# Weight units split in pairs of 2048 columns in the plain stages of a decoder layer

## What is computed

```python
h = x + 1/2 * post1(SwiGLU_1(pre1(x)))
u = pre_mix(h);  P = u @ W_in
m = (sig(g1)*y_gla + sig(g2)*y_gdn + sig(g3)*y_xa) @ W_out
h = h + post_mix(m)
h = h + 1/2 * post2(SwiGLU_2(pre2(h)))
```

## Time and profile before

| | us |
|---|---|
| time, median of 3 runs | 2432.47 |
| lowest and highest | 2431.55, 2433.93 |
| time of the profiled execution | 2433.06 |
| its span, first to last instruction | 2431.3 |
| busy PE / DVE / ACT / POOL | 2410.6 / 1840.5 / 1336.8 / 440.0 |

### The profile page before, as it was taken

How to read it: one execution, slowest core, us unless ns; L and a number is a source line. 1 busy time by engine, 2 the same in 40 slices (tenths; PEclk the granted TensorE clock), 3 DMA queues, 4 the chain that set the end, 5 groups by cost and what they waited for, 6 DMA issues and landing times.

```text
span 2431.3 us, 32326 instructions
## 1 busy us (share of the span) xinstructions
PE 2410.6 (99%) x10933; PEld 1998.5 (82%) x10933; DVE 1840.5 (76%) x2219; ACT 1336.8 (55%) x1613; POOL 440.0 (18%) x867
## 2 busy tenths in 40 slices
PE   8999999999999999999999999999999999999998
PEld 7888888888888888888888888888888888888886
DVE  6999999987566456677676464465689999998885
ACT  6555555554555556657575444444655555555553
POOL 5211212201222003223242020010112121121000
PEclk9999999999999999999999999999999999999999
DMA  7777767767778765555665677676667777676665
GB/s 243 213 215 214 221 207 218 213 208 223 226 240 257 199 188 157 170 160 159 170 183 159 200 208 195 211 238 191 209 207 220 211 215 217 208 223 211 197 204 193
DMA packets 306063, 498.53 MB, mean 205 GB/s; under 512 B 28460, under 2 KB 102320, under 8 KB 305200
## 3 DMA queue, kind: packets, MB, share of 16 engines
q1 hardware_dynamic: 282336, 457.85, 62.7%
q0 software_dynamic: 23344, 38.95, 5.0%
q10 hardware_dynamic: 288, 0.52, 0.1%
HBM read 471.39 MB, written 8.52 MB: 197 GB/s over the span
## 4 chain that ended last, share of the span: by engine, by line
PE 92%; POOL 2%; DMA 2%; DVE 2%; SPq 1%; issue 1%; ACT 0%; DVEq 0%; POOLq 0%; ACTq 0%
PE acc L770 40%; PE acc L858 39%; PE mix L858 9%; POOL mkh L733 1%; DMA sq<-mk_scratch 1%; POOL mkh L730 1%; PE acc L795 1%; DMA post_a<-n_ffn_post 1%; SPq L438 0%; SPq L472 0%; PE mix L1082 0%; DVE wlo L1971 0%; PE acc L813 0%; PE mix L831 0%; PE mix L1128 0%
## 5 line engine op out<-in xcount | busy, mean ns | idle before, releaser
L1289 ACT ACTIVATE whi<-raw 128x1024 fp32r<-128x1024 f32 x860 | 902.3, 1056 | 972.4 <-PE acc L770 480.0
L1823 DVE TENSOR_TENSOR wlo<-raw,whi 128x1024 fp32r<-128x1024 f32 x568 | 687.3, 1228 | 322.8 <-ACT whi L1289 312.2
L1971 DVE TENSOR_TENSOR wlo<-raw,whi 128x2048 fp32r<-128x2048 f32 x146 | 333.6, 2285 | 54.1 <-ACT whi L1289 54.1
L770 PE MATMUL acc<-whi,u_hi 128*128 128x512 f32 x896 | 356.9, 398 | 0.0
L770 PE MATMUL acc<-whi,u_lo 128*128 128x512 f32 x896 | 349.4, 390 | 0.0
L770 PE MATMUL acc<-wlo,u_hi 128*128 128x512 f32 x896 | 349.1, 390 | 0.0
L387 POOL DMA_DIRECT2D nat<-nat x416 | 203.5, 498 | 791.9 <-DVE nat L2058 649.0
L858 PE MATMUL acc<-whi,x_hi 128*128 128x512 f32 x860 | 334.7, 389 | 0.3 <-DVE nat L1926 0.3
L858 PE MATMUL acc<-wlo,x_hi 128*128 128x512 f32 x860 | 334.6, 389 | 0.0
L858 PE MATMUL acc<-whi,x_lo 128*128 128x512 f32 x860 | 334.6, 389 | 0.0
L770 PEld LDWEIGHTS acc<-whi,u_lo 128*128 128x128 f32 x896 | 168.2, 188 | 35.8
(11 more groups left out here) (476 smaller groups left out, 3848.7 us busy)
## 6 DMA issues: line engine op xcount, KB each, us to landing
raw<-w_ffn_gu SPq DMA_DIRECT2D x352, 512.0 KB
raw<-w_ffn_down SPq DMA_DIRECT2D x176, 512.0 KB
raw<-w_in SPq DMA_DIRECT2D x224, 256.0 KB
raw<-w_in SPq DMA_DIRECT2D x96, 512.0 KB
raw<-w_mem_kv SPq DMA_DIRECT2D x32, 512.0 KB
raw<-w_out SPq DMA_DIRECT2D x32, 512.0 KB
nat<-nat POOLq DMA_DIRECT2D x416, 32.0 KB, 3.5
raw<-w_in SPq DMA_DIRECT2D x64, 128.0 KB
```

What stands on the lines that cost most here:

```text
L770: ins = nc.tensor.matmul(acc[:, par, t, :], x[:, k0 + k, cols], w[:, k, :], start=first and k == 0 and m == 0, stop=last and k == UK - 1 a ...
L1289: act(whi[:, l % RING], raw[:, l], ACT.Copy).then_inc(hi_ready, 1)
L1823: tt(wlo[:, l], raw[:, l], whi[:, l % RING].bitcast(fp32), ALU.subtract).then_inc(lo_ready, 1)
L1971: tt(wlo[:, g:g + 2], raw[:, g:g + 2], whi[:, g % RING:g % RING + 2].bitcast(fp32), ALU.subtract).then_inc(lo_ready, 2)
```

## The change

On ACT, `split_two` is new: at every second slot (odd j) it waits for both loads and for `unit_used` of that slot, and makes the upper parts of two neighbouring units in one copy of 2048 columns. It is used at all slots of the plain stages, and in the pair stages for the pairs that are not sevens. At the even slots ACT now only does the tasks. On DVE the plain stages use `split_pair` at odd slots in place of `split` at each. The sevens stay single on both engines.

```diff
+            def split_two(n, per_i, j):
+
+                i, n0, per = per_i
+                if isinstance(n, int):
+                    l, loads = (n + LOOK) % RAW, (n + LOOK) // RAW + 1
+                else:
+                    l, loads = (n0 + j + LOOK) % RAW, i * (per // RAW) + ((n0 + j + LOOK) // RAW + 1)
+                for s in (l - 1, l):
+                    ac.wait_ge(raw_full[s], loads * LOADED)
+                ac.wait_ge(unit_used, n + 1)
+                act(whi[:, (l - 1) % RING:(l - 1) % RING + 2], raw[:, l - 1:l + 1], ACT.Copy).then_inc(hi_ready, 2)
+
             def slots(n0, i, per, tasks, until=None):
 
                 for j in range(per):
-                    if until is None or j + LOOK < until:
-                        split(at(n0, i, per, j), (i, n0, per), j)
+                    if j % 2 and (until is None or j + LOOK < until):
+                        split_two(at(n0, i, per, j), (i, n0, per), j)
                     tasks(j)
...
-                split(n, per_i, j)
+                if s is not None:
+                    split(n, per_i, j)
+                elif j % 2:
+                    split_two(n, per_i, j)
...
                 for j in range(per):
                     tasks(j)
-                    if until is None or j + LOOK < until:
-                        split(at(n0, i, per, j), j)
+                    if j % 2 and (until is None or j + LOOK < until):
+                        split_pair(at(n0, i, per, j), j)
...
             def split_pair(n, j):
 
-                g = (j + LOOK) % RAW - 1
+                g = ((n if isinstance(n, int) else j) + LOOK) % RAW - 1
```

## The result

The changed kernel takes **2516.06 us** (median of 4 runs, 2515.55 to 2519.5) against 2432.14 us of the kernel before (4 runs in the same rounds, 2431.55 to 2433.93): ratio 1.0345, 95% interval 1.0333 to 1.0357. That is 84 us slower, where 44.5 were forecast, and above the range. The profiled execution took 2519.5 us, its span 2517.8, 86.5 more than the span before; the trace is read against this number.

What follows compares the result with a forecast made beforehand. PE, busy 2410.6 of 2431.3 us, was taken as the bound, so each new PE wait is paid in full. Late pairs summed to 44.5 us on the profiled 2433.06, 2477.6, given as 2477 us; range 2455 to 2508.

Steps and rivals of the forecast that it cites:

- The question is whether a unit's lower part is still there when PE comes to it: Whole kernel: PE's new waits are paid in full; what ACT and DVE save in work is not the question.
- The latency of a pair, 4.50 of 5.44 us: Slots without tasks: pair ready 4.50 us after its slot is free, PE wants it at 5.44; spare falls 5.6 to 0.9.
- Busy time of DVE and ACT lower by some 45 and 75 us: Sign to look for in the whole trace: both engines less busy by these amounts, the span longer all the same.
- Mixer, slot 1, 12.8: Proj groups 1 to 3 and gates0: the pair behind the convolution 3.2 us late each time, 12.8 in all.
- `lower_turned`, 5.7: Second half of down1, two odd slots: the pair 2.8 us late at each, 5.7 in all.
- Mixture parts, 5.0: Slot 19 of up0 and up1, slot 7 of gates1: 1.7 us late each, 5.0 in all.
- The same holds for the 60 sevens of gu1 and gu2; cost nothing: Pair right behind each seven in gu1 and gu2: just in time, spare some 0.2 us, cost nothing.
- Sevens in the first halves of down, 7.3: First halves of down1 and down2: five places in each, 0.73 us late, 7.3 in all.
- Steps of slots 18, 20 and 22, 1.6, bounds 0 and 10: Mixers: DVE's tasks stand behind a pair and PE's next small step waits, 0.4 us a group, 1.6 in all.
- First chunks of gu1 and gu2, mem, out, 12.1: Slot 1 of gu1 and gu2 2.5 us each, 6.0 with gu1's slots 9 and 11; mem 3.4 and out 2.7 estimated.
- The clock falls: Rival, chance 0.13: six of the long PE waits bring half clock, some 3 us each, 18 more: 2495 us.
- The upper end takes in both slower rivals but not their sum: Range's upper end, 2508 us: covers more late steps (2501, chance 0.20) or the clock's fall (2495, chance 0.13).

Runs made afterwards that it cites:

- slot1_single: Changed kernel, but slots 0 and 1 of the four groups with a mixer split singly on ACT and DVE: 2501.37 us, ratio 1.0276.
- pair_first: Changed kernel with DVE's pair ahead of its task in five slots (lower_turned twice, mixture parts three times): 2501.06 us, ratio 1.0280.
- late_singles: Changed kernel with ACT's copy single at chunk ends of gu1 and gu2 and two pairs behind each seven of down's first halves: 2493.13 us.
- where_free: Kernel before, with pairs on both engines only in plain slots whose tasks leave time, 119 pairs: 2434.80 us, ratio 1.0009.
- dve_singles: Changed kernel, but in the plain stages DVE makes two single subtractions after the odd slot's tasks in place of a pair: 2486.87 us.
- hold8: Kernel before, with eight extra DVE additions ahead of the subtraction at four slots of proj group 0, to make PE wait: 2451.32 us.
- plain_only: The change in the plain stages alone, on ACT and DVE, with ACT single in the pair stages: 2487.74 us, ratio 1.0213.

## Why the prediction was wrong

The direction, the reason and the largest term were right; the sum was half of the loss, 42 us short. Of these, 12.8 are the half clock and 11.8 the chunk ends of gu1 and gu2, both of which the sum held at nothing; 8.1 the down halves, 6.0 the other steps of the mixers, 3.4 the first chunks with mem and out, 1.1 the mixture parts and `lower_turned`; slot 1 of the mixers came out 1.2 below. Two of the signs of being wrong that it named came true: PE waits in the chunks of gu1 and gu2 with sevens, and matmuls in mid-kernel stand 0.43 apart. By its own steps:

- *"The question is whether a unit's lower part is still there when PE comes to it"*: right. PE waits on lower parts for 49.2 us. Proj group 0 has no tasks and loses 0.00.
- *The latency of a pair, 4.50 of 5.44 us*: nearly right. The copy was 0.03 us longer and DVE's start behind it 0.07 later, so the spare is 0.8 and not 0.9 us. Small, but it is paid at each of some 50 places.
- *Busy time of DVE and ACT lower by some 45 and 75 us*: 24 and 57. ACT's saving per pair was 0.20 us and not 0.22; for DVE the sum was wrong, since only 206 of its 352 pairs are new and 0.17 us each make 35. None of it is on the path.
- *Mixer, slot 1, 12.8*: 11.6. `slot1_single` took it away, and with it the half clock that followed. *`lower_turned`, 5.7*: 5.7 and restarts. *Mixture parts, 5.0*: 5.2 and restarts. `pair_first` confirmed both.
- *"The same holds for the 60 sevens of gu1 and gu2; cost nothing"*: right of the sevens, and the first of the two steps that failed outright (the other is the half clock, below). I had looked at the pairs behind sevens and not at the pair at the end of a chunk, where ACT's silu waits for DVE's combination and the copy waits for the silu. 18 places of 0.53 with their restarts are 11.8 us in these two stages. `late_singles` took them away.
- *Sevens in the first halves of down, 7.3*: mis-sized. The five places are 0.95 each and not 0.73 (9.5 in all). I left out the waits at the start of each half (0.5, a chunk end, and 0.3) and 0.88 once more in each stage (in down1 at the end of the half, DVE's combination L2024 behind a pair; in down2 near the end of the kernel), 3.5 together, and the restarts.
- *Steps of slots 18, 20 and 22, 1.6, bounds 0 and 10*: 7.6, near the upper bound. "I cost them at nothing, cover being spares of 0.3 to 1.5 us" was too kind. A chain there goes from ACT to DVE and back several times, and a pair stands in the midst of it:

```profile
1094.41 0.48 DVE L2394 TENSOR_SCALAR xqT<-mix,blr 128x256 f32<-128x256 f32 x1 [2.71 <-ACT xqT L1657]
...
1094.81 2.33 DVE L1986 TENSOR_TENSOR wlo<-raw,whi 128x2048 fp32r<-128x2048 f32 x1
...
1096.14 0.42 ACT L1661 ACTIVATE xqT<-xqT 128x256 f32<-128x256 f32 x1
1097.06 0.88 DVE L2401 TENSOR_TENSOR_SCAN cb<-xqT 128x128 f32<-128x128 f32 x2
...
1101.41 0.71 PE L1160 MATMUL mix<-gqk 128*128 128x128 f32 x4 [0.40 <-DVE gq L2437]
```

  ACT was ready at 1096.56, the scan begins 0.5 later behind the pair, and PE waits 0.40 at the end of the chain. `where_free`, where slots 12 to 21 are single and so are 0 to 3 and the last two, loses 0 to 1.0 us a group, and `slot1_single` still loses 1.3 to 2.7: so most of the loss lies in slots 2, 3, 12 to 21 or the last two. That it is this chain in each group is read from the trace and was not tried alone.
- *First chunks of gu1 and gu2, mem, out, 12.1*: 15.5. Slot 1 of gu1 and gu2 lost 2.56 and 2.55, as forecast. mem lost 1.1 where 3.4 was estimated; the first two units of gu2 had waits of 1.5 and 1.9 that the sum does not have, and what holds them up was not looked into.
- *"The clock falls"*, a rival at 0.13 that the sum held at nothing, and the second step that failed: it came true beside the likeliest case. Nine waits, not six, brought it down, and each cost 1.4 to 1.6 us, not 3: 12.8 us in place of 18. The price was wrong because a stretch at half rate lasts 3.4 us here and gives 8 matmuls in place of some 15; it had been taken from the start of the kernel, where the matmuls up to 12.0 us stand 0.43 apart. The chance was wrong because I took "such waits stand between full stretches" as evidence against: the kernel before had one wait of 2.1 us to judge by. The Trainium skill (TensorE: Matmul & The Clock Gate, Why this matters for your kernels) says that pauses between bursts bring the clock down. It speaks of pauses longer than nearly all of those here; in these traces a fall followed 40 of 53 waits over 2 us already, and none of 88 of 0.8 to 1.5.
- *"The upper end takes in both slower rivals but not their sum"*: the error of the range. The two are not alternatives. Late steps make waits, and long waits bring the half clock; both happened, and a term was missing besides. The forecast with both prices would have been 2477 + 24 + 18 = 2519 us; that this is near 2516 is luck, since 11.8 us of the loss are in neither.

## What to carry to other kernels

Where PE is the bound, an operation of ACT or DVE is worth what its result's latency does to the spare of PE's next unit, not what it saves in busy time. Making two units in one operation raised that latency from 2.6 to 4.6 us and left it two units of PE's time in place of three, which took 4.8 us of a spare of 5.6. To price such an edit, list every place where a split stands behind a task that waits for another engine, at the ends of chunks and halves as well, and not only at the places with the longest tasks. In this kernel a PE wait over 2 us costs, beside its length, 1.6 us in three cases of four (an estimate of 1.2 us each from 40 of 53 waits), and to bring it under 2 us saves both, as `dve_singles` did.

## What the runs showed of the hardware that was not expected

- Half clock came in stretches of 3.4 us that cost 1.6 us each where matmuls of 512 columns filled them, began up to 1.5 us after PE had gone on again, and followed 39 of 52 waits of 2 to 3 us but not all: two waits of 3.0 us in one run (`hold8`) differed, and so did the same wait of 2.7 to 2.8 us in four kernels. The number of stretches also differs between executions of one kernel (`plain_only`: 2483 to 2492 us at a mean clock of 0.996 to 0.993).
- PE needs 0.1 us more to get going behind a wait: 0.33 us from the first matmul to the second, against 0.23.
- DVE started 0.10 us after the end of a copy of 2048 columns that it had waited for, and 0.03 us after one of 1024.
- Taking a copy out of an even slot let ACT's tasks there start 3.3 us sooner, since the copy had been waiting for PE. A wait for a free buffer holds up everything that stands behind it on the engine, and its removal is a gain that busy time does not show.
